# Linear attention with its heads two by two, and other slots for the work around it

## What is computed

```
# eight heads of softmax attention with forget gates, in blocks of 128 queries
s = where(causal, q @ k.T * scale + bias, -inf);  o_fox = softmax(s) @ v
# four heads of gated linear attention, keys 64 wide, values 128 wide, chunks of 64 tokens
attn  = where(tril, q_in @ k_in.T, 0)               # per chunk
kv    = k_st.T @ v                                  # per chunk
state = decay * state + kv                          # from chunk to chunk
o     = attn @ v + q_in @ state_before_the_chunk
o     = rmsnorm(o, g) * silu(g_r)
y = sigmoid(gate_fox) * (o_fox @ w_fox) + sigmoid(gate_gla) * (o @ w_gla);  out = y @ w_out
```

## Time and profile before

| | |
|---|---|
| median of three runs | 1055.09 us (1054.83 to 1055.9) |
| profiled execution | 1056.04 us, its span 1054.3 us |
| PE busy | 1046.2 us, 99% of the span |
| DVE busy | 816.1 us, 77% |
| ACT busy | 568.0 us, 54% |
| POOL busy | 44.7 us, 4% |
| chain that ended last | PE 91%, DVE 3%, ACT 2% |
| DMA | 121.28 MB, 115 GB/s over the span |

### The profile page before, as it was taken

One profiled execution on the slowest core, in us unless ns is written; L12 is line 12 of the kernel. 1 busy time (PEld: TensorE's weight loads), 2 busy tenths in 40 slices (PEclk: granted clock), 3 DMA queues, 4 the chain that ended last, 5 costly groups with the idle time before them and its releaser, 6 DMA issues.

```text
span 1054.3 us, 16505 instructions
## 1 busy us (share of the span) xinstructions
PE 1046.2 (99%) x6657; PEld 947.8 (90%) x6657; DVE 816.1 (77%) x971; ACT 568.0 (54%) x816; POOL 44.7 (4%) x98
## 2 busy tenths in 40 slices
PE   9999999999999999999999999999999999999997
PEld 7899999998888988888888999889899999998886
DVE  6998989989985583467689775558778878789964
ACT  6555455456654683567776344344454544566542
POOL 2000000000001310001000000021000000000001
PEclk9999999999999999999999999999999999999999
DMA  9623422451152553232120347315524224450052
GB/s 298 201 80 94 147 81 81 153 202 46 33 191 59 182 151 105 66 89 73 41 81 20 102 133 229 118 42 179 160 80 155 86 81 133 147 200 1 1 200 80
DMA packets 111835, 121.28 MB, mean 115 GB/s; under 512 B 6512, under 2 KB 92544, under 8 KB 111760
## 3 DMA queue, kind: packets, MB, share of 16 engines
q1 hardware_dynamic: 108544, 115.47, 34.3%
q10 hardware_dynamic: 2240, 2.11, 0.9%
q0 software_dynamic: 976, 2.66, 0.7%
HBM read 111.80 MB, written 6.29 MB: 112 GB/s over the span
## 4 chain that ended last, share of the span: by engine, by line
PE 91%; DVE 3%; ACT 2%; issue 1%; SPq 1%; DMA 1%; POOL 0%; ACTq 0%; DVEq 0%; POOLq 0%
PE bank L1961 13%; PE bank L1962 13%; PE bank L1960 13%; PE bank L1872 8%; PE bank L1862 5%; PE bank L2022 5%; PE bank L2023 5%; PE bank L2024 5%; PE bank L1864 5%; PE bank L1863 5%; PE bank L1927 1%; PE bank L1929 1%; PE bank L1928 1%; PE bank L2113 1%; PE bank L2112 1%
## 5 line engine op out<-in xcount | busy, mean ns | idle before, releaser
L1961 PE MATMUL bank<-tc,w_hi 128*128 128x256 f32 x576 | 163.3, 283 | 0.0
L1962 PE MATMUL bank<-tc,w_lo 128*128 128x256 f32 x576 | 163.3, 283 | 0.0
L1960 PE MATMUL bank<-tc,w_hi 128*128 128x256 f32 x576 | 163.2, 283 | 0.0
L1962 PE MATMUL bank<-u_hi,w_lo 128*128 128x256 f32 x504 | 142.9, 283 | 0.0
L1961 PE MATMUL bank<-u_lo,w_hi 128*128 128x256 f32 x504 | 142.8, 283 | 0.0
L1960 PE MATMUL bank<-u_hi,w_hi 128*128 128x256 f32 x504 | 142.8, 283 | 0.0
L1303 DVE TENSOR_TENSOR w_lo<-h,w_hi 128x1024 fp32r<-128x1024 f32 x72 | 87.8, 1222 | 33.6 <-ACT w_hi L765 33.6
L1962 PEld LDWEIGHTS bank<-tc,w_lo 128*128 128x128 f32 x576 | 110.8, 192 | 0.0
L1960 PEld LDWEIGHTS bank<-tc,w_hi 128*128 128x128 f32 x576 | 110.8, 192 | 0.0
L1961 PEld LDWEIGHTS bank<-tc,w_hi 128*128 128x128 f32 x576 | 110.8, 192 | 0.0
L1197 DVE TENSOR_TENSOR w_lo<-raw,w_hi 128x1024 fp32r<-128x1024 f32 x57 | 69.5, 1221 | 42.3 <-ACT w_hi L693 42.1
(11 more groups left out here) (313 smaller groups left out, 2511.1 us busy)
## 6 DMA issues: line engine op xcount, KB each, us to landing
raw<-in_w_in SPq DMA_DIRECT2D x28, 512.0 KB, 3.9
raw<-in_ffn_w_down SPq DMA_DIRECT2D x20, 512.0 KB, 6.5
h<-in_ffn_w_gate SPq DMA_DIRECT2D x9, 1024.0 KB, 5.5
h<-in_ffn_w_up SPq DMA_DIRECT2D x9, 1024.0 KB, 8.7
raw<-in_ffn_w_gate SPq DMA_DIRECT2D x9, 1024.0 KB, 5.4
raw<-in_ffn_w_up SPq DMA_DIRECT2D x9, 1024.0 KB, 8.1
h<-in_w_in SPq DMA_DIRECT2D x6, 1024.0 KB, 7.0
h<-in_ffn_w_down SPq DMA_DIRECT2D x8, 512.0 KB, 6.6
```

Of the source, the lines that this page charges most:

```text
L1960: mm(dst, w_hi[:, slot(u), w], moving(n, 0, k, sums), start=first and k == 0, stop=False, skip_group_check=True)
L1961: mm(dst, w_hi[:, slot(u), w], moving(n, 1, k, sums), start=False, stop=False, skip_group_check=True)
L1962: last = mm(dst, w_lo[:, slot(u), w], moving(n, 0, k, sums), start=False, stop=k == KD // 2 - 1, skip_group_check=True)
```

## The change

1. `WARM` goes from 9 to 32, the warm-up products shrink from 128x512 to 128x128, and DVE sets `mean_g` first instead of fourth.
2. `gla_steps` lists a pair's steps by kind, and PE works on both heads of a pair at once: the scores alternate between rows 0 to 63 and 64 to 127 of the array (one head each), and so do the products with the states; the key-value products go chunk by chunk. Each pair has one group of scores, one of key-value products and one of outputs.
3. The slots: both outputs of the first pair in slot 20, the means in 21 and 22 (before 20, 22, 22, 24); of the second pair the scores in 24, key-value products in 25, outputs in 28, means in 29 and 30 (before scores 24 and 25, key-value products 25 and 26, outputs 28 and 30, means 30 and 32).
4. ACT's copies of the means stand at the beginning of slots 22, 23, 30 and 31; all four copies of the second pair's scores stand in slot 25.
5. Weight splits: the ACT halves of five units go from slots 15, 18, 22, 26, 30 to 19, 23, 24, 27, 31, the DVE halves from 16, 19, 23, 27, 31 to 22, 24, 25, 30, 33. The gate products go from slots 25, 29, 33, 37 to 23, 27, 31, 35, and before the reciprocal. The low part of the second pair of softmax heads goes from slot 21 to 23, the third from 29 to 31.

The diff, without the parts that only move a line with its condition:

```diff
-WARM = 9
+WARM = 32
...
-            gla_steps += [("attn", 2 * j), ("attn", 2 * j + 1), ("kv", 2 * j), ("kv", 2 * j + 1),
-                          ("o", 2 * j), ("ms", 2 * j), ("o", 2 * j + 1), ("ms", 2 * j + 1)]
+            gla_steps += [(kind, 2 * j + e) for kind in ("attn", "kv", "o", "ms") for e in range(2)]
...
-        gla_slots = {13: (0,), 15: (1,), 17: (2, 3), 18: (4, 5), 20: (6,), 22: (7, 8), 24: (9, 10), 25: (11, 12),
-                     26: (13,), 28: (14,), 30: (15, 16), 32: (17,)}
-        gated_slots = {25: 0, 29: 1, 33: 2, 37: 3}
+        gla_slots = {13: (0,), 15: (1,), 17: (2, 3), 18: (4, 5), 20: (6, 7), 21: (8,), 22: (9,),
+                     24: (10, 11), 25: (12, 13), 28: (14, 15), 29: (16,), 30: (17,)}
+        norm_slots = {20: 0, 21: 1, 28: 2, 29: 3}
+        copy_slots = {17: (0, 1), 25: (2, 3)}
+        mean_slots = {22: 0, 23: 1, 30: 2, 31: 3}
+        gated_slots = {23: 0, 27: 1, 31: 2, 35: 3}
+        fox_rest_slots = {13: 0, 23: 1, 31: 2, 37: 3}
+        hi_slots = {19: 7, 23: 8, 24: 9, 27: 10, 31: 11}
+        lo_slots = {22: 7, 24: 8, 25: 9, 30: 10, 33: 11}
...
+                if sl in mean_slots:
+                    n = mean_slots[sl]
+                    act.wait_ge(gms_ready, n + 1)
+                    nc.scalar.activation(msq[:, n, :], gbank(gla_steps.index(("ms", n))), ACT.Copy).then_inc(ms_out, 1)
...
-                    mm(bank[:, 7, :], mean_g[:, :], c_neg[:, :], start=True, stop=True)
+                    mm(bank[:, 7, 0:P], mean_g[:, :], mean_g[:, :], start=True, stop=True)
...
+            def chunk_scores(j, *banks):
...
+                for t in range(TT):
+                    toks = slice(t * P, (t + 1) * P)
+                    for e in range(2):
+                        rows = slice(64 * e, 64 * e + 64)
+                        last = mm(banks[e][:, toks], arena[rows, T_GK + j, toks], arena[rows, T_GQ + j, toks],
+                                  start=True, stop=True)
+                        if t == TT - 1:
+                            last.then_inc(attn_ready, 1)
+
+            def chunk_states(j, *banks):
+
+                pe.wait_ge(kst_copied, 2)
+                pe.wait_ge(attn_copied, 4 * j + 4)
+                for c in range(NCH - 1):
+                    odd = c % 2
+                    rows = slice(CHUNK * odd, CHUNK * odd + CHUNK)
+                    for e in range(2):
...
+            def chunk_outputs(j, *banks):
+
+                pe.wait_ge(attn_masked, 4 * j + 4)
+                pe.wait_ge(state_ready, (NCH - 1) * (j + 1))
+                for e in range(2):
+                    n = 2 * j + e
+                    for t in range(TT):
+                        mm(banks[e][:, t * P:(t + 1) * P], arena[:, T_GV + t, n * GLA_DV:(n + 1) * GLA_DV],
+                           intra[:, e, t, :], start=t == 0, stop=False, skip_group_check=True)
+                for c in range(1, NCH):
+                    cols = slice(c * CHUNK, (c + 1) * CHUNK)
+                    for e in range(2):
+                        rows = slice(64 * e, 64 * e + 64)
+                        last = mm(banks[e][:, cols], state[rows, c, :], arena[rows, T_GQ + j, cols],
+                                  start=False, stop=c == NCH - 1, skip_group_check=True)
...
+                    elif kind == "ms":
+                        pe.wait_ge(on_ready, n + 1)
                         pe.wait_ge(sq_lo_out, n + 1)
```

More of the change, by code:

```diff
@@ L1088, in _ @@
                     nc.scalar.activation(ga, gb, ACT.Exp, scale=-1.0 / TAU).then_inc(a_act, 1)
+                if sl in norm_slots:
+                    n = norm_slots[sl]
+                    act.wait_ge(o_ready, n + 1)
+                    nc.scalar.activation(msq[:, n, :], o_bank(n), ACT.Square).then_inc(sq_ready, 1)
+                    act.wait_ge(sq_ready, n + 1)
+                    if n:
+                        act.wait_ge(gms_ready, n)
+                    nc.scalar.activation(sq_hi, msq[:, n, :], ACT.Copy).then_inc(sq_hi_out, 1)
                 for g in gla_slots.get(sl, ()):
@@ L1108, in _ @@
                                          scale=rinv[:, sl:sl + 1]).then_inc(probs_ready, 1)
-                if sl in FILLED:
-                    v = U_FILL + FILLED[sl]
-                    split(v + 4)
+                if sl in FILLED and FILLED[sl] not in hi_slots.values():
+                    split(U_FILL + FILLED[sl] + 4)
+                if sl in hi_slots:
+                    split(U_FILL + hi_slots[sl] + 4)
                 if sl - 1 in FILLED and FILLERS[FILLED[sl - 1]][0] == "k":
@@ L1522, in ffn @@
                     down_lo(layer, d)
+            V.memset(mean_g[:, :].bitcast(F32), 1.0 / GLA_DV).then_inc(hidden_ready, PAIRS)
             V.memset(eps_t[:, :], 4 * EPS).then_inc(merged, TILES)
@@ L2118, in _, with key_transposes @@
             pe.wait_ge(v_lo, TT)
-            read = {"kst": lambda n: (kst_copied, n + 1), "attn": lambda n: (attn_copied, 2 * n + 2),
-                    "kv": lambda n: (state_ready, (NCH - 1) * (n // 2 + 1)), "o": lambda n: (on_ready, n + 1),
-                    "ms": lambda n: (ms_out, n + 1)}
+            def key_transposes(g, n):
+                dst = gbank(g)
+                if n == 0:
+                    pe.wait_ge(gv_out, TT)
+                    pe.wait_ge(a_dve, 6)
+                else:
+                    pe.wait_ge(kst_copied, 1)
+                for t in (2 * n, 2 * n + 1):
+                    for j in range(2):
+                        c = (t % 2) * 2 * P + j * P
+                        last = nc.tensor.transpose(dst[:, c:c + P], arena[:, T_KST + j, t * P:(t + 1) * P], ident[:, :])
+                last.then_inc(kst_ready, 1)
@@ new lines, in chunk_states @@
+            def chunk_states(j, *banks):
+                pe.wait_ge(kst_copied, 2)
+                pe.wait_ge(attn_copied, 4 * j + 4)
[3 more added lines that the diff above has]
+                    for e in range(2):
+                        hh = 2 * j + e
+                        last = mm(banks[odd][64 * e:64 * e + 64, (c // 2) * P:(c // 2 + 1) * P],
+                                  kst_tok[rows, c // 2, hh * GLA_DK:(hh + 1) * GLA_DK],
+                                  arena[rows, T_GV + c // 2, hh * GLA_DV:(hh + 1) * GLA_DV], start=True, stop=True)
+                    if c >= NCH - 3:
+                        last.then_inc(kv_ready, 1)
@@ L2174, in _ @@
-                    if kind == "kv":
-                        j, part_n = n // 2, n % 2
-                        pe.wait_ge(kst_copied, 2)
-                        for c in range(part_n, NCH - 1, 2):
-                            rows = slice(CHUNK * part_n, CHUNK * part_n + CHUNK)
-                            for e in range(2):
-                                hh = 2 * j + e
-                                last = mm(dst[64 * e:64 * e + 64, (c // 2) * P:(c // 2 + 1) * P],
-                                          kst_tok[rows, c // 2, hh * GLA_DK:(hh + 1) * GLA_DK],
-                                          arena[rows, T_GV + c // 2, hh * GLA_DV:(hh + 1) * GLA_DV], start=True, stop=True)
-                        last.then_inc(kv_ready, 1)
```

104 lines of the change are left out of this document (34 added, 70 removed).

## The result

| | before | after |
|---|---|---|
| median | 1055.18 us (1054.56 to 1055.9, 6 runs) | 1061.49 us (1060.83 to 1062.15, 6 runs) |
| ratio | | 1.006, 95% interval 1.0047 to 1.0073 |
| profiled execution, its span | 1056.04, 1054.3 us | 1061.43, 1059.7 us |
| PE busy | 1046.2 us | 1045.9 us |
| start of the last product with the values | 539.45 us | 544.53 us |

The kernel is slower by 6.3 us, against a forecast of 1057.7 and a range up to 1060.0. The first slot's scores start 3.21 us later than before, slot 17's 3.17 later, and the last product with the values 5.09 later. So 3.2 us arise before the mixer's loop, where I had counted 1.0, and 1.9 inside it, where I had counted 1.6. Another 0.3 arise at the first filler behind that product, where I had counted nothing: it starts 0.52 us after the product (544.53 to 545.05), before the change 0.17 (539.45 to 539.62).

What follows compares the result with a forecast made beforehand. PE, busy 99% of the span, was taken as the bound. Work -5.9, means +4.7, key-value products and slot 28 +2.8, start +1.0 made +2.6 us: 1058.6 profiled, 1057.7 as median, range 1052.0 to 1060.0.

Steps and rivals of the forecast that it cites:

- PE's work: Scores, key-value products and outputs of both pairs: alternating heads and fewer groups take 5.9 us from PE.
- Means: Slots 21, 22, 29, 30: PE waits for the square's low part, 1.0 and 1.35 us per pair, 4.7 in all.
- Slot 25 and slot 28: PE waits 1.8 us for ACT's copies in slot 25, 1.0 for the exponential before slot 28; 2.8 together.
- The loop: Mixer's loop, slot 16 to the last product with the values: work, means and key-value waits together cost 1.6 us.
- Behind the loop: After the loop's last product: the rest of the program shifts with it, no further cost counted.
- The start: Warm-ups: first real product at 7.5 us, clock up at about 7.0 as before; costs 1.0 us, bounds 0 and 2.3.
- The load's time: Warm-ups at the start: at 107 ns per load, 32 end by 4.6 us, the start costs zero and the sum is 1.6.
- the late clock: Rival: the clock rises late, or slot 25's waits reach their upper bound; +3.9 to +5, 1059 to 1060 us; chance 0.12.

Runs made afterwards that it cites:

- The edit that moves them: Changed kernel with the old start and PE's four means one slot later (22, 23, 30, 31): 1054.76 us, ratio 0.9995 against the kernel before.
- The old slots: Changed kernel's alternation and groups by pairs, with the old start and, as far as possible, the slots of before: 1051.85 us, ratio 0.9964 against the kernel before.
- the rest alone: Changed kernel with the start of the kernel before (nine 128x512 warm-ups): 1057.43 us, ratio 1.0019 against the kernel before.
- the split moved: Changed kernel, its own start, unit 9's weight split moved from ACT's slot 24 to 25 and DVE's 25 to 26: 1059.01 us, ratio 1.0034 against the kernel before.
- the new start alone: Kernel before with only the changed start (32 warm-ups 128x128, constant matrix set first): 1058.56 us, ratio 1.0032.

## Why the prediction was too low

- **PE's work, right.** Forecast 5.9 us; the groups give 1.6, 0.9 and 3.6, some 6.1. Two parts were off and nearly cancel: I took the first pair's key-value products as unchanged, and they save 0.3; I took all four outputs at 2.76, and three of them took 2.68. The Trainium skill ("TensorEngine Tiling (Array Packing)", Key Properties) says that different tiles of the array can load and multiply in parallel; the trace agrees, 1.71 us alternating against 2.87.
- **Means, right.** Forecast 1.0 and 1.35, twice; measured 4.6 in all, 0.99 and 1.32 in the second pair. The chain through ACT and DVE, read off before's own order, held to a few hundredths. The edit that moves them gave back 2.7: two of the four waits, 1.8 us, and others behind them. The old slots removed all four.
- **Slot 25 and slot 28, right in place and nearly in size.** 1.9 for 1.8, 0.6 for 1.0. The exponential's wait shows only where the clock did not fall, and 0.4 in the repeat of the changed kernel. I left out that the clock can fall behind the long wait.
- **The loop without the fall of the clock:** +1.6 from slot 0 to the last product in the trace, for a forecast of +1.6.
- **Behind the loop, left out.** "The rest of the program hangs on the loop's last product and shifts with it": it shifts by 0.3 us more, at the first filler, which waits 0.24 for DVE's product of a gate. With the loop's 1.6 this makes most of the +2.05 of the medians.
- **The start, the step that failed.** "If PE goes from 1.2 to 2.4 GHz at about 7.0 as before": it does not. The price of a narrow warm-up was right (0.21 forecast, 0.215 measured), so the first real product came at 8.00. But I took the moment of the clock from the trace of before as if it were fixed, and it depends on what PE runs. Real work started 8.00 - 5.72 = 2.28 us later; the nine products until 11.90 took 3.90 us instead of 9 x 0.23 = 2.07, a loss of 1.8 where the kernel before loses 0.6; the sum is 3.5, of which 3.2 reach slot 0 (the wait at 28.83 takes the rest, as forecast). My upper bound of 2.3 failed too, since it let the clock rise no later than the last warm-up. The term was mis-sized by 2.2 us, and this alone takes 1057.7 to 1059.9, just inside my range. The last 1.6 us to 1061.5 are the 0.4 by which the rest alone (+2.05) exceeds the forecast +1.6, the 0.1 by which the kernel before now measures higher, and the remainder below. The number depends on the moment of the rise: over the five traces with this start slot 0 was 2.35 us (rise at 10.23) to 3.36 us (12.33) later than in the kernel before.
- **The load's time.** The trace has 0.215 us from one narrow product to the next at 1.2 GHz, so my estimate from the Trainium skill ("TensorE: Matmul & The Clock Gate", on LDWEIGHTS), 32 of them gone by 4.6 us, is not what happened. That does not refute the 107 ns that the Trainium skill gives for a load: a quarter of a 128x512 product's 0.43 us, my estimate for a narrow product alone, and 0.107 for a load in front of it give 0.215. The two load rows do not decide it either; whether the load itself is slower at the low clock stays open.
- **The remaining 0.7 to 1.1 us** (6.0 to 6.3 less 5.2) I put down to the fall of the clock behind slot 25's wait. From slot 0 to the last product with the values the changed kernel loses 1.9 and, in its repeat, 2.5 us, the one with the old start and no fall 1.6: 0.3 and 0.9 more. With the split moved there is no fall, and the loop takes the same time with either start (126.94 and 126.97 us), so the new start by itself does not lengthen it. Part of the remainder is the sum itself: the new start alone loses 3.33 us up to slot 0 but only 2.92 up to the last product, 0.4 that the changed kernel's loop does not give back. The parts are as small as the noise of the medians, and that the fall makes up the whole rest is not shown.
- Of the rivals, the late clock was the one that came true, at a higher price than the "+3.9 to +5" that I gave it.

## What to carry to other kernels

Short matmuls in large groups that alternate between halves of the array are a real gain, 6 us of PE's work here, of which alternating the rows is 3, and the larger groups and the order by chunks are the rest; moving their consumers closer at the same time cost more than that, since PE had nothing to put in the time between. Keep a mean, copy or state behind as much filler as ACT and DVE need after the transposes that feed them (3.8 us here, against 2.8 of filler); count the filler and not the slots, since a slot can be empty. Split a change into work and slots before judging it: the same work in the old slots was 3.6 us faster than the kernel before. Warm-up products of the same kind as the real ones served better here than short ones, and their cost must be counted until the clock is up, not until they end. An edit that lengthens a wait of PE can cost more than the wait, by the clock behind it.

## What the runs showed of the hardware

- The granted clock rose at 4.59 to 7.85 us with nine or sixteen warm-ups of 128x512, and at 9.65 to 12.33 with 20 or 32 of 128x128 that ran without a gap from 1.11 us; behind these it rose only after real 512-wide products had begun.
- Narrow products with a weight load each followed one another at 0.215 us at the low clock, half of a 128x512 one's 0.43 there, not a quarter.
- The clock can fall in the middle of a busy loop: to 0.5 for 3.4 us behind a wait of PE of 1.7 to 1.9 us, in three of five profiles, and by the recorded mean clocks in at least 9 of 35 executions of kernels with this wait, against 1 of 123 of the others. The same kernel had it in three executions of ten and not in the other seven.
- Two heads' 64-row products, 28 records, take 1.71 us in turns between the halves of the array's rows and 2.87 one head behind the other.
